# Eight stages of split-precision products on one core: three terms of a weight block made in passes, queries and keys turned two banks at a time, and other planner tables

## What is computed

```
for l in range(2):                                  # first block
    x = x + 0.5 * swiglu(rms_norm(x, ...), ffn1_w_gate[l], ffn1_w_up[l], ffn1_w_down[l])
    u = rms_norm(x, mix_norm[l]) @ w_in[l]          # z, xbc, dt, q_lat, kv_lat, k_pe, c_h, c_b, c_c
    y_ssd  = ssd_mixer(...)     # conv, both directions of a chunked scan, times silu(z), norm
    y_mla  = mla_mixer(...)     # 8 heads: latents -> q, k, v; norm, rope, softmax, norm
    y_conv = conv_mixer(...)    # gate * conv(gate * h), norm
    x = x + concatenate([y_ssd, y_mla, y_conv]) @ w_out[l]
    x = x + 0.5 * swiglu(rms_norm(x, ...), ffn2_w_gate[l], ffn2_w_up[l], ffn2_w_down[l])
for l in range(2):                                  # second block
    proj = rmsnorm(x) @ w_in_2[l]
    oa = diff_attention(q, k, v, lam)               # 8 heads, two maps each, causal
    hb = mlstm_chunkwise(mq, mk, mv, i_pre, f_pre)
    u  = sigmoid(ga) * (norm(oa) * silu(az) @ w_out_a) + sigmoid(gb) * (norm(hb) * ... @ w_out_b)
    x  = x + u @ w_o
```

## Time and profile before

| | before |
|---|---|
| median of 3 runs | 1864.54 us |
| the profiled execution's own time | 1864.64 us |
| its span in the trace | 1862.8 us |
| PE busy | 1847.7 us, 9674 matmuls |
| PEld busy | 1562.2 us |
| DVE busy | 1216.8 us |
| ACT busy | 1057.0 us |
| POOL busy | 107.2 us |
| granted TensorE clock | 1.00 over the whole span |

### The profile page before, as it was taken

The page is one execution under the profiler, slowest core; times in us unless marked ns, Lnnn a source line. Parts: engine busy times, 40 slices in busy tenths (PEclk is TensorE's granted clock), DMA queues, the critical chain, the costliest instruction groups (busy, mean ns, idle before and its releaser), DMA issues.

```text
span 1862.8 us, 24631 instructions
## 1 busy us (share of the span) xinstructions
PE 1847.7 (99%) x9674; PEld 1562.2 (84%) x9674; DVE 1216.8 (65%) x1872; ACT 1057.0 (57%) x1557; POOL 107.2 (6%) x85
## 2 busy tenths in 40 slices
PE   9999999999999999999999999999999999999999
PEld 7888998788888888899888888888878888888887
DVE  5654787865555555578876555587757478775845
ACT  5444677555444444476756444566776456667742
POOL 0000110000000000011000000001101000110100
PEclk9999999999999999999999999999999999999999
DMA  7555553335555555553334555554445555544553
GB/s 289 183 189 178 163 170 103 114 128 189 181 186 187 188 185 183 184 166 135 114 105 156 183 188 185 171 183 155 138 150 172 187 169 182 160 135 146 171 191 115
DMA packets 86579, 309.82 MB, mean 166 GB/s; under 512 B 9648, under 2 KB 10288, under 8 KB 86464
## 3 DMA queue, kind: packets, MB, share of 16 engines
q1 hardware_dynamic: 85680, 306.35, 49.4%
q0 software_dynamic: 496, 1.65, 0.2%
q10 hardware_dynamic: 288, 0.25, 0.0%
HBM read 307.16 MB, written 1.05 MB: 165 GB/s over the span
## 4 chain that ended last, share of the span: by engine, by line
PE 88%; DVE 6%; ACT 4%; issue 1%; POOL 1%; DVEq 0%; ACTq 0%
PE bank L1120 84%; PE bank L1117 4%; DVE WL L1970 2%; DVE XC L2120 1%; ACT WH L1518 1%; ACT PA L1518 1%; POOL STATS L2717 1%; ACT L1518 1%; ACT MP L1518 1%; DVE PA L2587 0%; DVE BO L2569 0%; DVE BO L2577 0%; ACT XC L1518 0%; DVE XBG L2097 0%; DVE STATS L2285 0%
## 5 line engine op out<-in xcount | busy, mean ns | idle before, releaser
L1970 DVE TENSOR_TENSOR WL<-RAW,WH 128x1024 fp32r<-128x1024 f32 x585 | 705.7, 1212 | 444.6 <-ACT WH L1518 439.9
L1518 ACT ACTIVATE WH<-RAW 128x1024 fp32r<-128x1024 f32 (+2 forms) x587 | 609.6, 1048 | 462.1 <-PE bank L1120 459.7
L1120 PE MATMUL bank<-WH,XTH 128*128 128x512 f32 (+1 forms) x1376 | 544.3, 396 | 0.5 <-DVE WL L1965 0.5
L1120 PE MATMUL bank<-WL,XTH 128*128 128x512 f32 (+1 forms) x1376 | 535.5, 389 | 0.0
L1120 PE MATMUL bank<-WH,XTL 128*128 128x512 f32 (+1 forms) x1376 | 535.2, 389 | 0.0
L1120 PE MATMUL bank<-WH,FR 128*128 128x512 f32 x1264 | 391.9, 391 | 0.0
L1120 PEld LDWEIGHTS bank<-WH,XTH 128*128 128x128 f32 x1376 | 258.5, 188 | 55.0 <-issue 3.4
L1120 PEld LDWEIGHTS bank<-WL,XTH 128*128 128x128 f32 x1376 | 258.3, 188 | 53.5
L1120 PEld LDWEIGHTS bank<-WH,XTL 128*128 128x128 f32 x1376 | 258.6, 188 | 51.8 <-issue 1.4
L1120 PEld LDWEIGHTS bank<-WH,FR 128*128 128x128 f32 x1264 | 234.0, 188 | 47.4
L1120 PE MATMUL bank<-WL,FR 128*128 128x512 f32 x632 | 247.1, 391 | 0.0
(11 more groups left out here) (317 smaller groups left out, 1626.3 us busy)
## 6 DMA issues: line engine op xcount, KB each, us to landing
RAW<-in_WALL_dram SPq DMA_DIRECT2D x569, 512.0 KB, 3.3
RAW<-in_WALL_dram SPq DMA_DIRECT2D x8, 448.0 KB, 3.3
RAW<-in_WALL_dram SPq DMA_DIRECT2D x8, 256.0 KB, 2.6
X<-in_x_dram SPq DMA_DIRECT2D x4, 256.0 KB, 5.1
out_dram<-X SPq DMA_DIRECT2D x4, 256.0 KB, 2.0
ROWP<-in_ROWP_dram POOLq DMA_DIRECT2D x1, 672.0 KB, 10.2
CONSTS<-in_CST_dram POOLq DMA_DIRECT2D x1, 664.0 KB, 7.8
ROUNDED<-in_CSTR_dram POOLq DMA_DIRECT2D x1, 208.0 KB, 12.9
```

The lines of the kernel that those rows point to most:

```text
L1120: return self.e.matmul(out, lhs, rhs, start=start, stop=stop, skip_group_check=True)
L1518: return self.e.activation(out, in_, func, **k)
L1970: self.e.tensor_tensor(lo, raw, hi.bitcast(F32), ALU.subtract).then_inc(*self.up("lo", j))
```

## The change

**Queries and keys.** The chain of the heads waits for four groups of two `qkt` phases in place of two groups of four, so that other work can be placed between them.

**Passes.** `PE.block` makes the terms of a block in three passes over its chunks and halves: first all xh·hi, then all xl·hi, then all xh·lo. It waits for `hi` at its start, for the high part of the left operand in the first pass, for the low part in the second, and for `lo` before the third. The last block of a projection does this half by half. Block 0 waits for `hi` of each of its two chunks and makes the low terms last.

**Planner.** `start` lets a block begin up to a third of its length before its left operand's low part is there, and two thirds before its own low part. `late_x` comes after block 1 and places one `split` before the flips. `WORK`, `HOP`, `LEAD` and `RULE` have other numbers.

```diff
-    "xsq": "A160", "rstd": "V41 G176", "rows_x": "V61", "rows": "P18 A80", ...
+    "xsq": "A160", "rstd": "V45 G193", "rows_x": "V61", "rows": "P14 A80", ...
...
-HOP = {"P": 15, "A": 6, "V": 11, "G": 45}
+HOP = {"P": 25, "A": 6, "V": 1, "G": 80}
...
-RULE = {"ffn": (0, 20, 40), "mix": (420, 120, 80), "hyb": (560, 60, 0)}
+RULE = {"ffn": (60, 240, 40), "mix": (420, 100, 80), "hyb": (500, 0, 20)}
...
     def late_x(self):
+        self.add("split", 2)
         for c in (4, 6):
             self.add("flip", "x", 0, c, 2)
-            self.add("split", c // 2)
+        self.add("split", 3)
...
+        third = self.length(lin, n) // (6 if n == len(lin.parts) - 1 else 3)
         for c in lin.parts[n]:
             ...
-            when = max(when, self.ends[phase])
+            when = max(when, self.halves[phase], self.ends[phase] - third)
...
-        return max(when, self.split_ends.get(len(self.blocks), NEVER))
+        j = len(self.blocks)
+        return max(when, self.hi_ends.get(j, NEVER), self.split_ends.get(j, NEVER) - 2 * third)
...
-        if j == 0:
+        if j == 1:
             self.late_x()
...
-            yield [("qkt", i, g) for g in range(0, 8, 2)]
-            yield [("qkt", i, g) for g in range(8, 16, 2)]
+            for g in range(0, 16, 4):
+                yield [("qkt", i, g), ("qkt", i, g + 2)]
...
     def block(self, j):
-        w.wait_ge(*(self.at("lo", j) if j else self.at("lo_first", 0)))
...
+        w.wait_ge(*self.at("hi", j))
+        whole = last and lin.kind != "thin"
+        for halves in ((0,), (1,)) if whole else ((0,),) if lin.kind == "thin" else ((0, 1),):
+            for x in passes:
+                if x == 2:
+                    w.wait_ge(*self.at("lo", j))
+                for n, c in chunks:
+                    if x == 0:
+                        self.left_hi_made(lin.src, c)
+                    elif x == 1:
+                        self.left_made(lin.src, c)
+                    for half in halves:
+                        m = self.products(lin, half, x, xh[:, c, :], xl[:, c, :], hi[:, n, :], lo[:, n, :], first and n == 0,
+                                          last and n == len(kk) - 1)
+            if whole and halves == (0,):
+                m.then_inc(*self.up("half", lin.key))
+        m.then_inc(*self.up("block", j))
...
-    def products(self, lin, half, xh, xl, hi, lo, st, en):
+    def products(self, lin, half, x, xh, xl, hi, lo, st, en):
+        left, right = (xl if x == 1 else xh), (lo if x == 2 else hi)
+        st, en = st and x == 0, en and x == 2
         if lin.kind == "tok":
-            o, s = ps[:, 0:lin.w], slice(128 * half, 128 * half + 128)
-            self.mm(o, xh[:, s], hi, st, False)
-            self.mm(o, xl[:, s], hi, False, False)
-            return self.mm(o, xh[:, s], lo, False, en)
+            return self.mm(ps[:, 0:lin.w], left[:, 128 * half:128 * half + 128], right, st, en)
```

More of the change, by code:

```diff
@@ L200 @@
 FREES = {"seg": "A", "as": "V"}
-HOP = {"P": 15, "A": 6, "V": 11, "G": 45}
+HOP = {"P": 25, "A": 6, "V": 1, "G": 80}
 LEAD = {
     "ffn": {
-        "sums": 40, "flips": 80, "evicted": 180, "steps": -20,
+        "sums": -180, "flips": 20, "evicted": 50, "steps": 180,
     },
     "mix": {
-        "qk": 70, "mla_head": 330, "rope1": -50, "decay": -50, "states": 100, "segment": -20, "finish": 60, "flips": -90,
-        "conv": 100, "conv2": -140, "evicted": 60, "sums": 30, "kpe": -300, "skip": -200, "heads": 100, "lat": 20,
+        "qk": 230, "mla_head": 360, "rope1": -50, "decay": -20, "states": 140, "segment": 30, "finish": -100, "flips": 300,
+        "conv": 100, "conv2": 60, "evicted": 300, "sums": -100, "kpe": 30, "skip": -20, "heads": 250, "lat": 20, "cn": -10,
+        "rows": 150,
     },
     "hyb": {
-        "hq": -100, "diff_head": 30, "sums": 30, "chain": 30, "hb_t": -200, "u": -250, "rows": 140, "hb": -100, "pair": 300,
-        "hconv": -10, "bz": 300, "evicted": 340, "flips": -130, "steps": 250, "oan": 110,
+        "hq": -270, "diff_head": 140, "sums": 60, "chain": -50, "hb_t": -130, "u": -30, "rows": 180, "hb": 200, "pair": 300,
+        "hconv": 180, "bz": 30, "evicted": 340, "steps": 30, "oan": 20,
     },
 }
-RULE = {"ffn": (0, 20, 40), "mix": (420, 120, 80), "hyb": (560, 60, 0)}
+RULE = {"ffn": (60, 240, 40), "mix": (420, 100, 80), "hyb": (500, 0, 20)}
 def plain(phase):
@@ L251, in __init__ @@
         self.ends, self.split_ends, self.owed, self.table = {}, {j: 0 for j in range(NSPLIT)}, [], None
+        self.hi_ends, self.halves = {j: 0 for j in range(NSPLIT)}, {}
         self.small, self.taken, self.empty = (6, 7), 0, {}
@@ L289, in add @@
                 first = since
+            if step[0] == "A":
+                self.halves[phase] = since
         for b in self.next_small(name):
@@ L426, in start, with length @@
             when = max(when, min(self.freed.get(p, 0) for p in free))
-        return max(when, self.split_ends.get(len(self.blocks), NEVER))
+        j = len(self.blocks)
+        return max(when, self.hi_ends.get(j, NEVER), self.split_ends.get(j, NEVER) - 2 * third)
+    def length(self, lin, n):
+        return max((272 if lin.kind == "tok" else 288) * len(lin.parts[n]) * lin.w // 1024, 60)
     def block(self, lin, when):
@@ L440, in block @@
         self.phases.append(("block", j))
-        self.at["P"] = when + max((272 if lin.kind == "tok" else 288) * size // 1024, 60)
+        self.at["P"] = when + self.length(lin, n)
         self.ends["block", j] = self.at["P"] + HOP["P"]
-        if j == 0:
+        if j == 1:
             self.late_x()
@@ L1141, in block @@
         xh, xl = k.left(lin.src[0])
-        w.wait_ge(*(self.at("lo", j) if j else self.at("lo_first", 0)))
-        if last and lin.kind != "thin":
-            for c in kk:
-                self.left_made(lin.src, c)
-            for half in range(2):
-                for n, c in enumerate(kk):
-                    m = self.products(lin, half, xh[:, c, :], xl[:, c, :], hi[:, n, :], lo[:, n, :], first and n == 0, n == len(kk) - 1)
-                m.then_inc(*(self.up("block", j) if half else self.up("half", lin.key)))
-        else:
-            for n, c in enumerate(kk):
-                if n and not j:
-                    w.wait_ge(*self.at("lo", 0))
-                self.left_made(lin.src, c)
-                for half in range(1 if lin.kind == "thin" else 2):
-                    m = self.products(lin, half, xh[:, c, :], xl[:, c, :], hi[:, n, :], lo[:, n, :], first and n == 0,
-                                      last and n == len(kk) - 1)
-            m.then_inc(*self.up("block", j))
+        chunks = list(enumerate(kk))
@@ new lines, in block @@
+        passes = (0, 1, 2)
+        if j == 0:
+            self.left_hi_made(lin.src, kk[0])
+            for n, c in chunks:
+                w.wait_ge(*(self.at("hi", 0) if n else self.at("hi_first", 0)))
+                for x in (0, 1):
+                    if x:
+                        self.left_made(lin.src, c)
+                    for half in range(2):
+                        self.products(lin, half, x, xh[:, c, :], xl[:, c, :], hi[:, n, :], lo[:, n, :], first and n == 0, False)
+            for n, c in chunks:
+                w.wait_ge(*(self.at("lo", 0) if n else self.at("lo_first", 0)))
+                for half in range(2):
+                    m = self.products(lin, half, 2, xh[:, c, :], xl[:, c, :], hi[:, n, :], lo[:, n, :], False, False)
+            m.then_inc(*self.up("block", j))
+            return
@@ L1162, in block, with left_hi_made @@
                 self.emptied[lin.pair[t]] = (by, (lin.key, t))
+    def left_hi_made(self, src, c):
+        name = src[0]
+        if name == "y" and c >= 12:
+            self.w.wait_ge(*self.at("cn_act", (src[1], "hi", c - 12)))
+            return
+        if name == "y":
+            name = "ys" if c < 8 else "mo"
+        self.w.wait_ge(*self.at("left_hi", (name, src[1], c // 2 * 2)))
     def left_made(self, src, c):
@@ L1176, in products @@
         if lin.kind == "tok":
-            o, s = ps[:, 0:lin.w], slice(128 * half, 128 * half + 128)
-            self.mm(o, xh[:, s], hi, st, False)
-            self.mm(o, xl[:, s], hi, False, False)
-            return self.mm(o, xh[:, s], lo, False, en)
+            return self.mm(ps[:, 0:lin.w], left[:, 128 * half:128 * half + 128], right, st, en)
         if lin.kind == "thin":
-            o = ps[0:16, 0:256]
-            self.mm(o, hi, xh, st, False)
-            self.mm(o, hi, xl, False, False)
-            return self.mm(o, lo, xh, False, en)
+            return self.mm(ps[0:16, 0:256], right, left, st, en)
         for f in range(2):
-            o, fs = ps[:, 256 * f:256 * f + 256], slice(256 * half + 128 * f, 256 * half + 128 * f + 128)
-            self.mm(o, hi[:, fs], xh, st and f == 0, False)
-            self.mm(o, hi[:, fs], xl, False, False)
-            m = self.mm(o, lo[:, fs], xh, False, en)
```

(2 more changed lines are left out.)

1 line of the change is left out of this document (added), and 40 rows, old and new, of the table WORK.

## The result

The changed kernel takes 1871.8 us, the median of 5 runs (1871.34 to 1873.29), against 1864.54 us of the kernel before (5 runs, 1864.51 to 1864.94): ratio 1.004, 95% interval 1.0029 to 1.0051. It is slower by 7.3 us, where 1.1 was forecast; the time lies 0.3 us above the range.

What follows compares the result with a forecast made beforehand. The prediction took the kernel as bound by PE's matmul stream, idle 0.8% of the span. Its terms, -0.4 - 1.0 - 0.4 - 0.6 + 5.0 - 1.0 - 0.5, summed to +1.1, so 1865.7 us, range 1857.5 to 1871.5.

Steps and rivals of the forecast that it cites:

- head: Program start: PE needs only the first half of block 0's high part, some given back before block 2; -0.4 us.
- queries and keys: Mixes: a block after every two `qkt` gives ACT time to empty the bank; QTK and QTQ waits go, -1.0 us together.
- heads: Heads of the mixes: changed places of `pt` shift the MP waits; -0.2 us per mix, -0.4 in all.
- `xs`: Mixes: `xs` moves about two blocks behind the conv output, so XC's wait of 0.6 us goes.
- scan: Scan of each mix: waits of 1.95 plus 1.0 at the end, less 0.4; about +2.5 us per mix, +5.0 in all.
- hybs: Differential attention: PT and PC waits fall from about 2.0 to 1.5 us per layer, -1.0 in all; gates another -0.5.
- the gates: Hybs: the gates are turned five blocks later, so their wait goes; -0.5 us.
- the long run: Scan: some 9 us without a block, 11 us of DVE work for 9 on PE; waits at five places, 1.95 us together.
- The sign that the prediction named: PE's busy time moving by more than 2 us at the same number of matmuls would mean their distance changed.
- The ceiling: Whole program: PE waits for a block's low part only at the head, so passes can directly win 0.5 us.
- The scan costs more: slower: Rival: in each mix another WH falls between exponential and `apply` at two of five places; sum +5.3, 1870 us; chance 0.17.
- The scan keeps its cover: Rival: DVE and ACT run ahead far enough before the long run; scan term 0 to -1.9, 1859 to 1861 us; chance 0.30.

Runs made afterwards that it cites:

- the run with the end moved: Changed kernel with, at each scan's end, the turned output's norm moved ahead of a split and both splits behind the flips: 1869.08 us, ratio 1.0023.
- fours: Changed kernel with the new tables, but queries and keys in two groups of four `qkt`: 1863.23 us, ratio 0.9992 to the kernel before.
- four runs with phases moved by hand: Scan's end moved in changed kernel, 1869.08 us; phases moved in kernel before with passes, 1869.52; block moved into changed kernel's long run, 1875.18; changed kernel's hybs' heads moved, 1875.70.
- the three groups: Changed kernel with the `qkt` in three groups (two, two and four) in place of four groups of two: 1871.75 us, ratio 1.0037 to the kernel before.
- phases moved in it: Kernel before with the passes; `fin_y` moved ahead of the flips in the mixes, a split and `ap` 7 moved in the hybs: 1869.52 us, ratio 1.0027.

## Why the prediction was wrong

By stretch, against the profiled execution of the changed kernel (7.8 us longer in its span):

| | forecast | measured |
|---|---|---|
| head | -0.4 | 0.0 |
| mixes: queries and keys, heads, `xs`, scan | +3.0 | +5.4 |
| hybs | -1.5 | +2.4 |
| ffn stages | 0 | 0.0 |

**The step that failed is the hybs.** Forecast -1.0 and -0.5 for the gates; measured: PC from 1.5 to 3.3, PT from 1.5 to 2.2, IFT 0.5 to 0.6, so +2.6 of waits. The prediction had `at` 6 at about 1.2 (it was 1.0) and `at` 1 at 0.3 (0.64), and put PT's wait at nothing without giving a reason. It is held up by a table load, the two evictions of BZ and a WH on ACT, 3.6 us that weren't walked; with BZ, its product and the split moved behind, PT's wait was gone. The gates' turn, five blocks later, waited just the same. By the stretches the hybs are 3.9 of the 6.7 us that are missing in the sum. The new tables made these waits: they are at 1.6 and 1.5 with the old ones.

**The mixes cost 2.4 more than forecast.** 0.9 is the clock in mix 4 and 0.6 is ZS, a wait at the head of a weight block; neither was walked. Heads: -0.2 for -0.4. XC and QTK/QTQ went as said.

**The scan: the size came near, and only half of the mechanism was right.** Forecast: +5.0, of it 1.95 per mix in the long run and 1.0 at the end. Right was the end: a WH ahead of the norm holds up the flips, shown by the run with the end moved, which gives back 0.9 in mix 1. Wrong was the run. The prediction let DVE's queue fall behind, 11 us of work for 9 on PE, with waits at five places. There is one wait with a row in each mix, 0.92, and both DVE and ACT had been idle before it. What it lacks is work for PE between a `seg` and its `apply`, and a block moved in took the wait away. The waits of the scan grew by 3.7 in all, 1.3 less than forecast; what brings the mixes over the forecast is PE's busy time, 3.1 more, of which the clock explains 0.9. Short waits are part of the rest: the records of neighbours overlap, so PE counts as busy in them. The four RS,SPREAD matmuls at 359.70 and at 366.99 last 1.45 us each time, for 0.70 and 1.38 at the two places before (with fours they take as long, so they don't tell the two lists apart). How the rest divides stays open, and that +5.0 was near is in part luck.

**The sign that the prediction named.** It said that more than 2 us of busy time would mean another distance of matmuls. It was 3.1, and the distance is unchanged: the two ffn stages between the mixes take 386.65 us in both kernels, and the growth is all in the mixes.

**Where the loss in the mixes comes from wasn't seen.** The prediction took the pairs as a gain of 1.0 with a term of their own, and the scan as another term. Fours with all else unchanged gave 8.6 us back, so pairs and scan are one term: blocks put between `qkt` are missing later, one of them in the scan. The pairs' price is +8.6, not -1.0.

**The head** was forecast at -0.4; PE started at 8.25 in place of 8.81 and gave it back with 0.6 for XTH.

**The ceiling.** "The passes have 0.5 us to win" is near for the list before (1.3 measured, with an interval that takes in none; 1.5 at the head in the profiled execution). It is wrong for the changed list, where they are worth 5.4 us. The prediction priced the passes against the old waits; their worth depends on the list.

**The rivals.** "The scan costs more: slower" is what the time says, but by another way: the waits of the scan stayed under its term, and hybs and busy time made the rest. "The scan keeps its cover" is what fours did. What stays open: a gain of pairs whose blocks come from elsewhere than heads and scan wasn't tried, and which of the planner's numbers makes the hybs' order isn't known.

## What to carry to other kernels

Where one engine is busy 99% of the time, the filler between its dependent phases is the scarce thing, and where it stands counts as well as how much of it there is: with fours and the new tables the scan has two blocks fewer than before and each mix is 1.8 us shorter. A wait of 0.3 us closed with a block of 2.7 us takes that block from a later place, so price such a step by what the last user of the filler loses. Walk the list to the end of the stage, on ACT and DVE as well: each queue's order decides, and what is moved out of one wait's way can stand in another's, as in three of the four runs with phases moved by hand. And a planner's tables should be judged with the rule they were made for: here the new tables were worth 10.4 us with the new rule, and the new rule without them cost 10.3.

## What wasn't expected of the hardware

PE's clock fell after short waits close together, though not each time. In the changed kernel PE waited 0.47 and 1.21 us within 2.3 us at 984 us, and the granted clock was 0.84 and then 0.73 over the next 8 us, that is, a stretch at 1.2 GHz before it was at 2.4 again; the same waits at 389 and 391 us left it at 1.00. With the three groups it fell in both places. It cost 0.9 us where it fell. In the kernel before, a single wait of 0.94 at the same place left it at 1.00; with phases moved in it, a wait of 3.13 brought it down in both mixes. The Trainium skill ("Perfetto Trace Analysis", section "Matmul Optimizations") says that it is important that matmuls run back to back, since the engine scales its power with use; the trace agrees so far as each of these falls comes with such waits, and puts a price on it. All five timed runs of the changed kernel had a mean clock of 0.998 or 0.999, those of the kernel with the scan's end moved 1.00.
